# Retrieval layer of a hybrid decoder block on one core: three of four token blocks through a dense product instead of gathered rows

## The reference

```python
# x: 512 tokens x 1024, float32; one layer
def peer(x, w_query, sub_keys, expert_u, expert_v):     # 16384 experts, u and v rows of 1024
    q = (xt @ w_query).reshape(T, 8, 2, 128)
    s = einsum('thcd,hckd->thck', q, sub_keys)          # 8 heads, 2 halves, 128 keys
    top_s, top_i = top_k(s, 16)
    cand_s = top_s[:, :, 0, :, None] + top_s[:, :, 1, None, :]
    cand_i = top_i[:, :, 0, :, None] * 128 + top_i[:, :, 1, None, :]
    best_s, pos = top_k(cand_s, 16)
    expert_idx, gate = take(cand_i, pos), softmax(best_s)        # 8 x 16 experts per token
    h = gelu(einsum('cd,ced->ce', x, expert_u[expert_idx]))
    return einsum('ce,ced->cd', gate * h, expert_v[expert_idx])

def reference(x, ...):
    mix = hybrid_mixer(x, w_in, ...)     # 4 retention heads, 4 differential attention heads, w_out
    x = layer_norm(ALPHA * x + mix, ln1_g, ln1_b)
    return layer_norm(ALPHA * x + peer(x, ...), ln2_g, ln2_b)
```

## Time and profile before

| | |
|---|---|
| median of 3 runs | 1660.17 us (1654.67 to 1662.5) |
| span of the profiled execution | 1633.5 us |
| what lies around the span, against the median | 26.7 us |
| PE busy | 1276.5 us, 78% |
| DVE busy | 1155.6 us, 71% |
| ACT busy | 267.2 us, 16% |
| POOL busy | 625.2 us, 38% |
| DMA moved | 603.44 MB, mean 369 GB/s |

### The profile page before, as it was taken

The page is one execution under the profiler, slowest core; times in us unless marked ns, Lnnn a source line. Parts: engine busy times, 40 slices in busy tenths (PEclk is TensorE's granted clock), DMA queues, the critical chain, the costliest instruction groups (busy, mean ns, idle before and its releaser), DMA issues.

```text
span 1633.5 us, 11511 instructions
## 1 busy us (share of the span) xinstructions
PE 1276.5 (78%) x3448; PEld 618.1 (38%) x3448; DVE 1155.6 (71%) x2727; ACT 267.2 (16%) x754; POOL 625.2 (38%) x645
## 2 busy tenths in 40 slices
PE   7879979888646994586978687878777878787885
PEld 5465446433323562232323233333333333332332
DVE  1349999767798979987676767776767677764454
ACT  0110000121211111121212121212121212121111
POOL 0004344474445565543434343434342434343320
PEclk9989999999767997798888888989897989899899
DMA  9939798897759898999999999999999999999993
GB/s 339 390 140 353 280 344 312 319 409 274 263 189 335 319 373 329 410 422 421 422 421 421 422 422 421 422 421 422 421 422 421 422 421 422 421 422 421 421 422 127
DMA packets 125710, 603.44 MB, mean 369 GB/s; under 512 B 12624, under 2 KB 14928, under 8 KB 76368
## 3 DMA queue, kind: packets, MB, share of 16 engines
q0 software_dynamic: 92160, 536.91, 81.2%
q1 hardware_dynamic: 33488, 65.80, 11.0%
HBM read 600.57 MB, written 2.10 MB: 369 GB/s over the span
## 4 chain that ended last, share of the span: by engine, by line
DMA 38%; PE 31%; DVE 23%; issue 3%; POOL 2%; SPq 1%; ACT 1%; DVEq 0%; POOLq 0%
DMA arena<-uv,idx 37%; PE W L474 7%; PE W L509 7%; DVE arena L1060 5%; PE ACC L474 4%; DVE xs L1052 4%; PE W L744 3%; PE W L716 3%; PE ACC L461 2%; POOL arena L438 2%; PE W L515 2%; DVE arena L1039 1%; DMA arena<-w_in 1%; DVE cand L1301 1%; DVE cand L1303 1%
## 5 line engine op out<-in xcount | busy, mean ns | idle before, releaser
L474 PE MATMUL W<-arena,fdiag 128*128 128x512 f32 x1024 | 498.9, 648 | 170.1 <-ACT fdiag L979 170.1
L426 POOL DMA_INDIRECT arena<-uv,idx x384 | 367.5, 957 | 586.7 <-PE W L474 355.7
L1060 DVE SCALAR_TENSOR_TENSOR arena<-arena,X 128x1024 f32<-128x1024 f32 x256 | 309.2, 1219 | 200.8 <-DMA arena<-uv,idx 199.7
L438 POOL DMA_INDIRECT arena<-uv,idx x256 | 257.3, 1005 | 372.2 <-DVE idx L1311 125.1
L474 PEld LDWEIGHTS W<-arena,fdiag 128*128 128x128 f32 x1024 | 208.6, 208 | 459.7 <-issue 253.0
L474 PE MATMUL ACC<-arena,fdiag 128*128 128x512 f32 x512 | 254.9, 660 | 69.3 <-ACT fdiag L979 69.3
L1060 DVE SCALAR_TENSOR_TENSOR arena<-arena,W 128x1024 f32<-128x1024 f32 x128 | 154.8, 1219 | 95.8 <-DMA arena<-uv,idx 95.4
L474 PEld LDWEIGHTS ACC<-arena,fdiag 128*128 128x128 f32 x512 | 107.0, 213 | 217.2 <-issue 132.1
L979 ACT ACTIVATE fdiag<-ident,gate 128x128 f32<-128x128 f32 x384 | 123.3, 390 | 354.7 <-DVE gate L1067 351.0
L1039 DVE SCALAR_TENSOR_TENSOR arena<-arena,X 128x1024 f32<-128x1024 f32 x128 | 150.0, 1216 | 24.8 <-DMA arena<-uv,idx 24.3
L509 PE MATMUL W<-arena 128*128 128x512 f32 x320 | 143.7, 605 | 9.7 <-DMA arena<-w_in 9.0
(11 more groups left out here) (178 smaller groups left out, 824.7 us busy)
## 6 DMA issues: line engine op xcount, KB each, us to landing
arena<-w_in SPq DMA_DIRECT2D x13, 2048.0 KB, 13.8
arena<-peer_w_query SPq DMA_DIRECT2D x8, 2048.0 KB, 14.4
arena<-uv,idx POOLq DMA_INDIRECT x640, 25.4
arena<-w_out SPq DMA_DIRECT2D x4, 2048.0 KB, 14.9
arena<-w_in SPq DMA_DIRECT2D x4, 512.0 KB, 6.4
out<-xs SPq DMA_DIRECT2D x4, 512.0 KB, 8.1
arena<-xT SPq DMA_DIRECT2D x1, 1536.0 KB, 18.2
xs<-x SPq DMA_DIRECT2D x1, 1536.0 KB, 17.0
```

What stands on the lines that cost most here:

```text
L426: pool.indirect_dma_start(out=fused[slot], out_offset=None, in_=uv, in_offset=bass.IndirectOffsetOnAxis(ap=idx[:, E + n:E + n + 1], axis=0 ...
L438: pool.indirect_dma_start(out=ring[:, r, :], out_offset=None, in_=rows, in_offset=bass.IndirectOffsetOnAxis(ap=idx[:, e:e + 1], axis=0), e ...
L474: last = nc.tensor.matmul(sum_of(b)[:, half * HW:(half + 1) * HW], fdiag[:, n % ND, :], fused[n % NS][:, D + half * HW:D + (half + 1) * HW ...
L1060: STT(out=fused[slot][:, 0:D], in0=fused[slot][:, 0:D], scalar=1.0, in1=token_of(b), op0=ALU.mult, op1=ALU.mult, accum_out=hid[:, E + n:E ...
```

## The change

The two waves become one: `fill_psum` runs 28 fills, `DQ` and `DKK` now 512 wide, and weights are loaded once except `w_query`. All four blocks go through `attend` and `mixed_out`. Block 0's queries are computed beside heads of blocks 1 and 2, and two of its retrieval units stand between heads of blocks 2 and 3.

Blocks 1 to 3 no longer gather. For each of `NT` = 128 tiles of 128 experts, `up(n)` multiplies the tile's u rows (a new input `uT`, laid out by tile) with the 384 tokens, ACT's `hidden(n)` applies Gelu, DVE's `mask_hidden(n)` multiplies by a gate matrix that is zero where a token did not pick the expert, and `add(n, d)` multiplies it with the tile's v rows for each of the three blocks. The gate matrix is built by `quad(q)`: for each token a product of two one-hot 128 x 128 matrices (`b_hot`, `a_hot`) that DVE's `hot_quads(d)` writes from the picks, after `turn_picks(d)` transposed them; ACT copies it out (`take_quad`), and it goes to a DRAM tensor `gd` and comes back by `load_g`. The first `NH` = 47 `up` tiles run before the dense loop: 23 right after the query product and 24 between the quads.

Block 0 keeps gathers, with a ring of `RING` = 6 rows of 4 KB, 128 dots and 128 sums all on DVE; 68 of the dots stand before the dense loop, after retrieval units, and the others in it.

```diff
-WAVES = [[0], [1, 2, 3]]
-NF = (NB - 1) * E
-FG = 4
+W_SLOTS = [0, 1, 2, 3, 0, 1, 2] + [0, 1] + [3, 2, 3, 2] + [0, 1, 0, 1]
+RING = 6
+ND = NB - 1
+TD = ND * P
+NT = P
+NH = 47
+UR = 4
+VR = 4
+LEAD = 6
+TAIL = 4
+WEIGH = 36
+QUADS = P // 4
+OH_RING = 4
+OH_BANKS = 5
+UP_FIRST = NH - ND * QUADS // 4
...
 # SP
+            def load_u(n):
+                if n >= UR:
+                    sp.wait_ge(u_ready, n - UR + 1)
...
+                sp.dma_start(u_ring[n % UR], uT[n].rearrange("p (k e) -> p k e", k=KD)).then_inc(u_landed[n % UR], 16)
+            def load_v(n):
+                if n >= VR:
+                    sp.wait_ge(v_done, n - VR + 1)
+                sp.dma_start(v_ring[n % VR], uv[n * P:(n + 1) * P, D:2 * D]).then_inc(v_landed[n % VR], 16)
+            def load_g(g):
+                if g >= 2:
+                    sp.wait_ge(masked, GT * (g - 1))
+                src = gd[:, :, g * GT:(g + 1) * GT, :].rearrange("c j i t -> j c (i t)")
+                sp.dma_start(g_ring[g % 2], src).then_inc(g_landed[g % 2], 16)
...
 # POOL
+            for s in range(ROWS):
+                e = s % E
+                if s < E and e % QUARTER == 0:
+                    pool.wait_ge(experts_ready, e // QUARTER + 1)
+                if s >= RING:
+                    pool.wait_ge(row_used[s % RING], s // RING)
                 pool.indirect_dma_start(
+                    out=ring[s % RING], out_offset=None, in_=rows,
...
 # PE
-            def add_rows(j):
-            def add_pairs(b):
+            def up(n):
+                pe.wait_ge(u_landed[n % UR], 16 * (n // UR + 1))
+                if n >= 2:
+                    pe.wait_ge(h_ready, n - 1)
+                for k in range(KD):
+                    last = nc.tensor.matmul(X[:, n % 2, 0:TD], u_ring[n % UR][:, k, :], actT[:, k, P:S],
+                                            start=(k == 0), stop=(k == KD - 1))
+                last.then_inc(u_ready, 1)
+            def quad(q):
+                pe.wait_ge(hot_ready, q + 1)
...
+                for m in range(4):
+                    last = nc.tensor.matmul(bank[:, m * P:(m + 1) * P], b_hot[:, q % OH_RING, m, :],
+                                            a_hot[:, q % OH_RING, m, :], start=True, stop=True)
+                last.then_inc(quad_ready, 1)
+            def add(n, d):
+                for half in range(2):
+                    last = nc.tensor.matmul(sum_banks(d)[:, half, :], h_slot(n)[:, d * P:(d + 1) * P],
+                                            v_ring[n % VR][:, half * HW:(half + 1) * HW],
+                                            start=(n == 0), stop=(n == NT - 1))
...
+            project()
+            score(0, 0)
+            for b in range(NB):
+                attend(b)
+                mixed_out(b)
+            turn_x1(NB - 1)
+            query()
+            pe.wait_ge(scores_stored, 4 + ND * WQ)
+            for n in range(UP_FIRST):
+                up(n)
+            for d in range(ND):
+                turn_picks(d)
+                for q in range(d * QUADS, (d + 1) * QUADS):
+                    quad(q)
+                    if q % 4 == 3:
+                        up(UP_FIRST + q // 4)
+            pe.wait_ge(quad_taken, ND * QUADS)
+            for n in range(NT - TAIL):
+                pe.wait_ge(masked, n + 1)
+                pe.wait_ge(v_landed[n % VR], 16 * (n // VR + 1))
+                for d in range(ND):
+                    last = add(n, d)
+                last.then_inc(v_done, 1)
+                if n + NH < NT:
+                    up(n + NH)
...
 # ACT
+            for n in range(UP_FIRST):
+                hidden(n)
+            for d in range(ND):
+                take_picks(d)
+                for q in range(d * QUADS, (d + 1) * QUADS):
+                    take_quad(q)
+                    if q % 4 == 3:
+                        hidden(UP_FIRST + q // 4)
+            for n in range(NH, NT):
+                hidden(n)
...
 # DVE
+            def dot(s):
+                STT(out=ring[r], in0=ring[r], scalar=1.0, in1=xs[:, 0, :], op0=ALU.mult, op1=ALU.mult,
+                    accum_out=hid[:, s:s + 1]).then_inc(row_used[r], 1)
+            def norm_picks(d):
+                dve.wait_ge(pk_exp_ready, d + 1)
...
+            def hot_quads(d):
+                dve.wait_ge(pT_ready, d + 1)
+                for q in range(d * QUADS, (d + 1) * QUADS):
+                    if q >= OH_RING:
+                        dve.wait_ge(quad_ready, q - OH_RING + 1)
+                    for m in range(4):
+                        t = 4 * (q % QUADS) + m
+                        TS(b_hot[:, q % OH_RING, m, :], iota_f[:], pT[d % 2][:, 1, t:t + 1], None, ALU.is_equal)
+                        last = TS(a_hot[:, q % OH_RING, m, :], iota_f[:], pT[d % 2][:, 0, t:t + 1],
+                                  pT[d % 2][:, 2, t:t + 1], ALU.is_equal, ALU.mult)
+                    last.then_inc(hot_ready, 1)
+            def mask_hidden(n):
...
+                TT(out=h, in0=h, in1=g_ring[g % 2][:, :, n % GT * CHUNK:(n % GT + 1) * CHUNK],
+                   op=ALU.mult).then_inc(masked, 1)
...
+            best_experts(0, 2)
+            retrieve(0, 3)
+            rows(8)
+            for s in range(4):
+                retrieve(1, s)
+                rows(5)
+            best_keys(2, 0)
+            norm_picks(0)
+            best_pairs()
+            best_experts(2, 0)
+            hot_quads(0)
+            for s in range(1, 4):
+                retrieve(2, s)
+                rows(6)
+            best_keys(3, 0)
+            norm_picks(1)
+            best_pairs()
+            best_experts(3, 0)
+            hot_quads(1)
+            for s in range(1, 4):
+                retrieve(3, s)
+                rows(6)
+            norm_picks(2)
+            rows(4)
+            hot_quads(2)
+            for n in range(LEAD):
+                mask_hidden(n)
+            for n in range(NT):
+                if n + LEAD < NT:
+                    mask_hidden(n + LEAD)
+                if n == WEIGH:
+                    weigh()
+                if n < WEIGH:
+                    rows(min(2, E - taken[0]))
+                else:
+                    rows(2 - n % 2)
...
+            for d in range(ND):
+                join_sums(d)
+                finish(d + 1)
```

More of the change, by code:

```diff
@@ new lines, in key_scores_0, with query @@
+            def key_scores_0(s):
+                pe.wait_ge(query_taken, s + 1)
+                if s >= 2:
+                    pe.wait_ge(scores_stored, s - 1)
+                for i in range(4):
+                    last = nc.tensor.matmul(X[:, s % 2, i * P:(i + 1) * P], qq0[:, s % 2, i, :],
+                                            keys[:, 4 * s + i, :], start=True, stop=True)
+                last.then_inc(keys_scored, 1)
+            def query():
+                pe.wait_ge(x1_taken, 2 * NB)
@@ L752, in query @@
+                        last.then_inc(query_ready, 1)
+                    pe.wait_ge(query_taken, 4 + 4 * (s + 1))
+                    for j in range(ND):
+                        n = 4 + s * ND + j
+                        if n >= 6:
                             pe.wait_ge(scores_stored, n - 1)
@@ L873, in attention, with project @@
-            def attention(b, beside):
+                    dst = {RV: rv, DV: dv, DQ: dqT, DKK: dkT}[g][:, part, :]
+                    nc.scalar.activation(dst, bank, ACT.Copy).then_inc(proj_taken_act, 1)
+                if n and FILLS[n - 1][0] in (RQ, RK):
+                    take_rotated(rots(n) - 1)
+            def project():
+                for n in range(len(FILLS)):
+                    take_fill(n)
+                    if n == fills_of(RV)[0]:
+                        act.wait_ge(lam_dots_ready, 1)
+                        nc.scalar.activation(lam[:, 2:4], lam[:, 0:2], ACT.Exp).then_inc(lam_exp_ready, 1)
@@ L882, in attention @@
                     last.then_inc(exps_ready, 1)
[L883 to L886 removed]
+                    beside(b, h)
                     act.wait_ge(a_turned, n + 1)
@@ new lines, in store_scores, with query @@
+            def store_scores(b, s, bank):
+                act.wait_ge(keys_scored, 4 + ND * s + b if b else s + 1)
+                nc.scalar.activation(scores[b][:, s * HW:(s + 1) * HW], bank, ACT.Copy).then_inc(scores_stored, 1)
+            def query():
+                for n in range(4, 20):
+                    s, i = divmod(n - 4, 4)
+                    act.wait_ge(query_ready, n + 1)
+                    if s and i == 0:
+                        act.wait_ge(keys_scored, 4 + s * ND)
+                    nc.scalar.activation(qq[:, i, :], W[:, 2 + n % 2, 0:TD], ACT.Copy).then_inc(query_taken, 1)
+                    if i == 3:
+                        for j in range(ND):
+                            store_scores(1 + j, s, W[:, (s * ND + j) % 2, :])
@@ new lines, in _ @@
+            project()
+            for b in range(NB):
+                attention(b)
+                take_mixed(b)
```

(6 more changed lines are left out.)

1119 lines of the change are left out of this document (430 added, 689 removed).

## The result

The changed kernel takes 2164.89 us (median of 4 runs, 2164.34 to 2167.15), beside 1658.34 for the kernel before on the same chip (the three runs given above and a fourth): ratio 1.305, 95% interval 1.302 to 1.308. It is 30% slower; the prediction said 2195, between 2120 and 2300. The profiled execution took 2164.58 us for a span of 2162.8.

A forecast was written before the change was run, and what follows sets the result against it. DMA gathers bound 959 of the old 1633.5 us; PE's dense work, 1849 us in sum, would replace them. Stages put the loop at 1079, plus 1077 to 2156, end 2169; with 1660.17 - 1633.5 added, 2195 us, range 2120 to 2300.

The forecast's parts named there:

- The offset: Added to the 2169 us span to get a time: 1660.17 - 1633.5, old median less old profiled span.
- The price of a float32 product: On PE at full clock: 0.859 us for 512 columns, 0.645 for 384, 0.224 for 128; two records each.
- Projection and attention: Ahead of the tiles: projection ends at 224 us, queries start at 460 and end at 557, tiles at 676.
- The queued exponential: ACT's exponential, behind hidden(22), holds up norm_picks(0) on DVE; the one-hot stage starts at 690 us.
- The one-hot stages: Ahead of the loop: DVE binds, 9.0 us per four quads against PE's 8.75; about 71 us a stage.
- a one-hot instruction above 0.35 us: In the one-hot stages, a sign of being wrong; assumed were 0.26 us for b_hot, 0.30 for a_hot.
- PE binds the stage: One-hot stages by the skill's formula: 33 us of DVE, PE's 8.75 binds, total changes by under 10 us.
- The gaps: Between one-hot stages: 85 us until the second, 76.5 until the third, with PE idle 70 us in each.
- The loop and the end: Dense loop starts at 1079 us, 10 after the third stage, takes 1077 to 2156; the end is at 2169.
- The bound of before: Old kernel, 664 to 1623 us: 959 us of gathers bound by DMA, 99% busy at 413 GB/s.
- DMA would be hidden in the dense loop: Dense loop: 2.3 MB in 10.3 us, 223 GB/s against 413 seen, so transfers are hidden.

The follow-up runs named there:

- the second trace: The kernel before, unchanged, run once more for another trace: 1655.56 us in one run, span 1653.8.
- The bfloat16 run: Changed kernel with bfloat16 operands in both dense-layer products, and TAIL from 4 to 1: 1726.67 us, ratio 1.042 to the kernel before.
- The run with the exponential alone: Changed kernel with block 1's picks' exponential and turn moved earlier, all 23 tiles still ahead of the first quad: 2147.20 us.
- two-product: Changed kernel with the third block's second product computed for expert tile 0 alone: 1968.23 us in one run.
- both edits: Changed kernel with bfloat16 products, tiles spread over the gaps and block 0's 40 dot products moved into the dense loop: 1715.45 us, ratio 1.035.

## Why the prediction was right, and where it was off

The mechanism and the sign were right: the dense product costs more PE time than the gathers cost DMA time. The miss is 2195.7 - 2164.9 = 30.8 us, inside the range, and most of it is no term of the change.

**The offset, 24.9 us of the 30.8.** The step that failed is the last sum, "2169 + (1660.17 - 1633.5)", and the sentence behind it, that the profile stands for the median. Execution and span differ by 1.8 us in every run of either kernel whose span is on record; the other 24.9 us were a difference between executions of the kernel before, of which the second trace shows 20.3, nearly all in its front. The changed kernel did not inherit it: its four times lie within 2.8 us.

**The price of a float32 product: right.** 5.16 us for eight of 384 columns, 5.15 for six of 512, 10.31 for a tile, as summed. The bfloat16 run shows how much of it is the type. The Trainium skill ("FP8 and Floating Point Precision", TensorE Precision Notes) says that a true float32 product makes four passes through the array; the factors 3.9 and 4.0 agree, and each of the two records would stand for two passes; the runs show only the times. The 131 ns that the skill ("TensorE: Matmul & The Clock Gate", Back-to-back issue gap) gives for 512 columns is met by no run here: 215 ns in bfloat16 is the least.

**Projection and attention: right.** Second fill at 16.04 (17), end of the projection at 223.1 (224), queries at 456.90 (460), 557 and 676 as forecast. The 557 holds some luck: the queries began 3 us early, and their first step took 26.9 us instead of 24.2, partly at the lower clock.

**The queued exponential: right.** `norm_picks(0)` on DVE waited 96.8 us in one piece for ACT (below), the one-hot tiles began at 689.57 (690). The run with the exponential alone puts its price at 17.7 us.

```profile
DVE gsum L1180 <- ACT both_uses L871: 96.8, 1, 96.8
```

**The one-hot stages: sized too high.** The step "I take 0.26 for `b_hot` and 0.30 for `a_hot`" gave DVE 9.0 us for four quads, and DVE would have bound. Start to start they are 0.20 and 0.25:

```profile
838.50 0.28 DVE L1193 TENSOR_SCALAR arena<-iota_f,both_uses 128x128 f32<-128x128 f32 x1
838.70 0.34 DVE L1194 TENSOR_SCALAR lng<-iota_f,both_uses 128x128 f32<-128x128 f32 x1
838.95 0.28 DVE L1193 TENSOR_SCALAR arena<-iota_f,both_uses 128x128 f32<-128x128 f32 x1
```

16 x 0.45 = 7.2 us, so PE binds with its 8.74, and DVE's stage is 755.15 - 689.57 = 65.6 us instead of 71. The second stage with its gap is 140.6 instead of 147.5. The third, up to the end of PE's last `up`, is 75.2 (75.5). The prediction's own sign for this, a one-hot instruction above 0.35 us, was badly chosen: the group's mean is 358 ns, yet the next instruction starts 250 ns later, since durations overlap. Only the steps tell that DVE does not bind. The formula of the Trainium skill that the prediction weighed ("VectorE: DVE Perf Modes", the errata note; 0.127 us by it, an estimate) is too low by 36 to 49%, and the same section says itself that it comes out too low. Its consequence, that PE binds the stage, is what happened, though the terms ahead of the loop then moved by 15.4 us and not by under 10.

**The gaps: right.** 755.15 to 838.50 is 83.4 (85), and 904.00 to 979.13 is 75.1 (76.5). PE's idle time in them was the cheapest thing to win back, and the prediction named it without drawing that.

**The loop and the end.** PE stands for 9.2 us between its last `up` and the first dense product (10):

```profile
1049.05 5.33 PE L664 MATMUL X<-arena 128*128 128x384 f32 x16
...
1063.56 6.51 PE L691 MATMUL W<-arena 128*128 128x512 f32 x8 [9.19 <-DMA arena<-uv]
```

The write of the last gates had begun at 1049.87, beside that `up`. All terms ahead of the loop sum to -15.4: start 1063.6, not 1079. The loop up to the last four tiles is 1064.1 (1056.6): the first tile took 13.4 us, starting at a granted clock of 0.50 (from 1063.56 to 1066.6), and a v tile was 4.3 us late at 2123, once `up` had run out. The end is 35.2 from there (33.3). So the span is 6 below 2169.

**The bound of before: right, and tested.** With half the bytes the stretch of gathers shrank to PE's pace. That DMA would be hidden in the dense loop held (211 GB/s), but with the cover gone, in the two-product and bfloat16 runs, it was the next limit at once.

## What to carry to other kernels

Before a gather of few rows is replaced by a dense product over all of them, price the product by the records of its own type: in float32 the 128 tiles cost 1320 us of PE against 959 us of gathers. In bfloat16 they leave transfers as the limit, and that alone is not a win either (1.042, 1.035 with both edits); only with the gates in bfloat16 and eight tiles to a transfer does the change win (0.934 and 0.931). Work that can stand anywhere belongs where its engine would be idle: 23 tiles computed early had left PE with nothing in two gaps, and to spread them brought 76 us beyond what the exponential cost. When you go from a span to a time, take the distance of each execution's span from its own time, not from the median of others.

## What the runs showed of the hardware

Transfers: with float32 gates among tiles of 4 KB rows (62576 packets under 2 KB in the run) the DMA engines showed 94 to 96% busy at 339 to 342 GB/s; with eight bfloat16 tiles to a transfer, pieces of 512 bytes as before but 37744 such packets, the mix ran at 400. A high DMA share thus was no proof of the ceiling in bytes. In the loops at 340 GB/s a transfer of 384 KB in 256-byte pieces took 19.7 us to land (median of 7), about what 768 KB in 512-byte pieces took (21.8, median of 6).

TensorE's clock: it held 1.00 (2.4 GHz) over 1060 us of unbroken work, and fell to means of 0.52 to 0.58 in the stretches where PE waited for DVE; in the bfloat16 loop, with PE busy for half the time, the mean was 0.73 to 0.78. Right after a wait, at a granted clock of 0.50 (from 1128.0 to 1130.9 us), four bfloat16 products of 512 columns took 1.86 us; 4 us later, at 0.98, they took 0.86.
